# Five of the six slabs of the first in-projection by one level of Strassen's scheme, with the weight sums on GpSimd

## The chip, the cores and the metric

One Trainium2 chip, one of its cores. The metric is the device time of one execution of the whole kernel in microseconds (us). All data are float32.

## The reference, cut to what matters

One hybrid block: an input projection, two mixers (differential attention and a gated delta rule), a merge, 16 experts, and then a second block. The change touches only the first products of the input projection:

```
h = rmsnorm(x, norm1_w)              # 512 tokens x 1024
p = einsum('bsd,dn->bsn', h, w_in)   # w_in: 1024 x 9248
qa, ka, va = p[:, 0:1024], p[:, 1024:2048], p[:, 2048:3072]
qa = apply_rope(qa); ka = apply_rope(ka)     # t*cos + rot(t)*sin
# differential attention over qa, ka, va follows
```

## The kernel before, in words

The kernel is a row of blocks (`nc.Block`), each with a hand-written instruction order for every engine. Between two blocks all engines meet at a barrier. Inside a block an engine waits only on semaphores.

The first block (lines 241 to 414) makes `hT`, the normed input with the model dimension on the partitions (8 tiles `k` of 128, each 512 tokens wide), and the projections to `qa`, `ka` and `va`. The list `UNITS1` (line 239) has 24 units of work. A unit makes one 128 x 512 tile of output in a PSUM bank by 8 accumulating matmuls. The weights come as slabs of 1024 x 512 (2 MB), four units to a slab, six slabs in all: the first half of `va` (slab 4, four units), then `qa` and `ka` (slabs 0 to 3, sixteen units), then the second half of `va` (slab 5, four units). Two more slabs (6 and 7) are only loaded here, for the next block. The `v` units (line 328) hold a slice of `hT` as the stationary operand and stream 512 columns of the weights; the `qk` units (line 331) hold the weights and stream the 512 tokens of `hT`.

A float32 matmul is two passes in the trace: each has its own weight load (LDWEIGHTS) and its own MATMUL record, so a unit is 16 passes.

- TensorE takes the units in turn through four banks, `PS[n % 4]`. Unit n waits until the bank was emptied four units ago (`proj_evac`, line 312), and for its slab (line 315).
- ScalarE empties a bank into `raw` (line 366) or `va` (line 362). For `qk` it also copies the tile with the 32-row halves exchanged into `turned`, in four copies (line 368).
- VectorE makes the rotary form with three `tensor_tensor` instructions per unit (lines 407, 409, 411).
- GpSimd has four memsets at the start (line 292) and nothing else in this block. Its next work comes hundreds of us later.
- The DMA queue of SyncE loads slabs into four slots (`slab(i % 4)`). Slab i, from the fifth on, waits until the slot's units are done (line 285).

The next block (lines 437 to 604) is the attention. Its first matmul (line 455) needs `qT` and `kT`. Semaphores that are no longer used are collected in `spent`, cleared by GpSimd at the start of a later block (line 1448) and handed out again.

Of the kernel before, what the change touches and what calls it, by code (L numbers as in the profile page):

```python
# [110 lines left out]
def build(nc, io):  # L111
    ctx = ExitStack()
    counts = {}
    with ctx:
# [96 lines left out]
        def slab(slot, k=KD, cols=512):  # L211
            return SLB[slot][:, 0:k * cols].rearrange("p (k n) -> p k n", k=k)
# [20 lines left out]
        cosT, sinT = R[5][:, 0:S], R[5][:, S:2 * S]  # L233
        raw = [R[5][:, 1024 + i * S:1024 + (i + 1) * S] for i in range(2)]
# [4 lines left out]
        UNITS1 = [("v", 0, t) for t in range(NT)] + [("qk", u // 4, u) for u in range(NQK)] + [("v", 1, t) for t in range(NT)]  # L239
        SLABS1 = [4, 0, 1, 2, 3, 5, 6, 7]  # L240
        with nc.Block() as block:
            @block.sync
            def _(sp):
# [51 lines left out]
            def _(pe):  # L295
                def turn(t):
                    pe.wait_ge(tile_scaled, t + 1)
                    if t >= 2:
                        pe.wait_ge(hT_low, t - 1)
                        pe.wait_ge(hT_high, t - 1)  # L300
                    for k in range(KD):
                        m = pe.transpose(PS[4 + 2 * (t % 2) + k // 4][:, k % 4 * P:(k % 4 + 1) * P], hn[:, t, k * P:(k + 1) * P], ident)
                        if k % 4 == 3:
                            m.then_inc(tile_turned, 1)

                pe.wait_ge(ident_in, 16)
# [3 lines left out]
                for n, (kind, i, u) in enumerate(UNITS1):  # L310
                    if n >= 4:
                        pe.wait_ge(proj_evac, n - 3)
                    bank_ = PS[n % 4]
                    if n:
                        pe.wait_ge(slab_in[n // 4 % 4], 16 * (n // 16 + 1))
                    w = slab(n // 4 % 4)
                    if kind == "v":
                        if i == 0:
                            pe.wait_ge(hT_low, u + 1)
                        for k in range(KD):  # L320
                            if i == 0 and k == 4:
                                pe.wait_ge(hT_high, u + 1)
                            if n == 0 and k == 0:
                                pe.wait_ge(first_half, 16)
                            if n == 0 and k == 4:
                                turn(1)
                                pe.wait_ge(slab_in[0], 16)
                            m = pe.matmul(bank_[:, :], hT[:, k, u * P:(u + 1) * P], w[:, k, :], start=(k == 0), stop=(k == KD - 1))
                    else:
                        for k in range(KD):  # L330
                            m = pe.matmul(bank_[:, :], w[:, k, u % 4 * P:(u % 4 + 1) * P], hT[:, k, :],  # L331
                                          start=(k == 0), stop=(k == KD - 1))
                    m.then_inc(proj_done, 1)
                    if n < 2:
                        turn(n + 2)
                    if n == 8:
                        pe.wait_ge(rows_in, 16 * 7)
                        pe.transpose(PS[6][:, 0:120], rows[0:120, 0:P], ident[0:120, 0:120])
                        pe.transpose(PS[7][:, 0:30], rows[0:30, P:2 * P], ident[0:30, 0:30]).then_inc(vec_t, 1)
                pe.wait_ge(tab_in, 16)  # L340

            @block.scalar
            def _(act):
# [13 lines left out]
                for t in range(1, NT):  # L357
                    tile(t)
                for n, (kind, i, u) in enumerate(UNITS1):
                    act.wait_ge(proj_done, n + 1)  # L360
                    if kind == "v":
                        a(nc.scalar.activation(va[:, u, i * 512:(i + 1) * 512], PS[n % 4][:, :], ACT.Copy), proj_evac)
                        continue
                    if u >= 2:
                        act.wait_ge(rope_done, u - 1)
                    a(nc.scalar.activation(raw[u % 2], PS[n % 4][:, :], ACT.Copy), proj_evac)
                    for q in range(4):
                        a(nc.scalar.activation(turned[u % 2][32 * q:32 * q + 32, :], raw[u % 2][32 * (q ^ 1):32 * (q ^ 1) + 32, :], ACT.Copy),
                          raw_turned if q == 3 else None, q == 3)
                    if n == 9:  # L370
                        act.wait_ge(vec_t, 1)
# [6 lines left out]
            def _(dve):  # L378
# [18 lines left out]
                for t in range(1, NT):  # L397
                    scale(t)
                    weigh(t)
                dve.wait_ge(bc_in, 16 * 8)  # L400
# [4 lines left out]
                for u in range(NQK):  # L405
                    dve.wait_ge(proj_evac, NT + u + 1)
                    v(nc.vector.tensor_tensor(t1, raw[u % 2], cosT, ALU.mult))
                    dve.wait_ge(raw_turned, u + 1)
                    v(nc.vector.tensor_tensor(t2, turned[u % 2], sinT, ALU.mult))
                    dst = qT[:, u, :] if u < HEADS else kT[:, u - HEADS, :]  # L410
                    v(nc.vector.tensor_tensor(dst, t1, t2, ALU.add), rope_done)
                dve.wait_ge(lam_exp, 1)
# [227 lines left out]

        cut = [wab_[:, i * P:(i + 1) * P] for i in range(2)]
        with nc.Block() as block:
            @block.sync
            def _(sp):
# [731 lines left out]
        def expert_slab(eng, r):  # L1376
# [18 lines left out]
            for k in range(4):  # L1395
# [3 lines left out]

        spent.extend([proj_done, proj_evac, raw_turned, rope_done, score_done, max_ready,  # L1400
                      exp_done, pd_ready, pT_done, pT_ready, pv_done, oT_evac, rstd2, sq_ready, ss_done, norm_done,
                      cf_done, cf_evac, wab_in, ab_done, ab_evac, p3_done, conv_done, silu_done, sq3, ss3, rstd3, qk_norm,
                      tr3, tr3_evac, *pre.values(), *piece_in, first_done,
# [1229 lines left out]
```

## Time and profile before

| what | value |
|---|---|
| median of 3 runs | 2372.22 us (2370.93 to 2374.9) |
| span of the profiled execution | 2369.5 us |
| TensorE busy, share of the span | 93% |
| VectorE, ScalarE, GpSimd busy | 37%, 23%, 7% |
| first block, until the attention's first matmul | 181 us |

The page gives the span of the profiled execution alone, which runs from its first to its last instruction. The lowest of the three timed runs is 1.4 us above it, and their median 2.7 us. In a timeline row of the trace the first number is the start in us from the start of the span, the second how long the merged group lasts. MATMUL records overlap: one starts before the one before it has left the array, so the time that a pass costs is the distance between starts and not its own length.

### The profile page before, as it was taken

Reading aid. Unit: us, or ns where it says so; the run is one execution under the profiler, and the core shown is the slowest. Engines: PE = TensorE matmul, PEld = TensorE weight load, DVE = VectorE, ACT = ScalarE, POOL = GpSimd, SP = SyncE. Lnnn points to the kernel's source line nnn. Section 1 sums busy time; section 2 is a strip of 40 time slices with the busy share of each in tenths; the row PEclk is TensorE's granted clock in tenths of the full one; section 3 lists DMA queues with packets and bytes.
Section 4 is the critical chain, followed back from the end, with each engine's and each line's share of the span. In section 5 each row is a group of like instructions: output and inputs, shape, how many; then the busy total and the mean of one; then the engine's idle time right before and its main releaser. Section 6 shows DMA issues by size and latency. Waiting matters only on the chain. (4 is left out here: it accounts for less than half of the span.)

```text
span 2369.5 us, 28558 instructions
## 1 busy us (share of the span) xinstructions
PE 2211.2 (93%) x11793; PEld 1112.4 (47%) x11793; DVE 880.0 (37%) x1559; ACT 535.8 (23%) x1000; POOL 170.2 (7%) x166
## 2 busy tenths in 40 slices
PE   8999999999999999979999888888888888999998
PEld 4445554467777754434333333333333324455544
DVE  2327757665777640240101010101010102456764
ACT  2435645532222241010000000000000002233323
POOL 0000000043433300000000000000000000022000
PEclk9999999999999999989999999999999999999999
DMA  6212110011011152438999999999999997221210
GB/s 245 71 36 74 36 36 18 9 37 37 20 28 37 29 181 78 171 122 332 428 428 428 428 427 427 428 428 428 428 427 428 428 427 304 76 72 36 76 54 36
DMA packets 94115, 488.07 MB, mean 206 GB/s; under 512 B 9957, under 2 KB 36995, under 8 KB 68899
## 3 DMA queue, kind: packets, MB, share of 16 engines
q1 hardware_dynamic: 93987, 486.25, 50.7%
q8 instruction: 94, 1.54, 0.3%
q14 instruction: 34, 0.28, 0.0%
HBM read 482.82 MB, written 3.41 MB: 205 GB/s over the span
## 5 line engine op out<-in xcount | busy, mean ns | idle before, releaser
L1576 PE MATMUL PS<-R 128*64 128x512 f32 x1024 | 232.3, 601 | 31.9 <-DMA R<-w_up 24.6
L1576 PE MATMUL PS<-SL,R 128*64 128x512 f32 x1024 | 227.2, 595 | 25.7 <-DMA SL<-w_gate 17.8
L2069 PE MATMUL PS<-HT,SL 128*128 128x512 f32 x384 | 168.6, 594 | 0.0
L1768 DVE TENSOR_TENSOR HT<-HT,PS 128x512 f32<-128x512 f32 x32 | 20.6, 683 | 369.8 <-PE PS L1576 369.8
L1576 PEld LDWEIGHTS PS<-R 128*64 128x64 f32 x1024 | 70.6, 138 | 182.2 <-issue 127.5
L1576 PEld LDWEIGHTS PS<-SL,R 128*64 128x64 f32 x1024 | 72.6, 137 | 177.8 <-issue 128.1
L1605 PE MATMUL PS<-SL,HT 128*64 128x512 f32 x256 | 114.4, 594 | 14.7 <-issue 6.0
L1605 PE MATMUL PS<-R,HT 128*64 128x512 f32 x256 | 114.3, 594 | 12.5 <-ACT HT L1693 7.0
L1773 DVE COPY HT<-PS 64x512 f32<-64x512 f32 x16 | 10.9, 684 | 304.8 <-PE PS L1606 304.8
L1606 PE MATMUL PS<-SL,HT 128*64 128x512 f32 x256 | 114.9, 596 | 0.0
L1606 PE MATMUL PS<-R,HT 128*64 128x512 f32 x256 | 114.8, 595 | 0.0
L669 PE MATMUL PS<-HT,SL 128*128 128x512 f32 x256 | 113.9, 599 | 0.8 <-PEq L437 0.8
L2069 PEld LDWEIGHTS PS<-HT,SL 128*128 128x128 f32 x384 | 72.2, 190 | 87.2 <-issue 86.1
L961 PE MATMUL PS<-HT,X 128*128 128x512 f32 x256 | 112.5, 592 | 0.0
L1688 ACT ACTIVATE HT<-PS 128x512 f32<-128x512 f32 x32 | 17.4, 595 | 415.5 <-PE PS L1576 415.5
L331 PE MATMUL PS<-HT,SL 128*128 128x512 f32 x256 | 110.3, 592 | 0.0
L1895 POOL MEMSET R<- 64x512 f32 x1 | 0.5, 519 | 1163.1 <-POOLq L1405 1163.1
L331 PEld LDWEIGHTS PS<-HT,SL 128*128 128x128 f32 x256 | 48.6, 190 | 60.8 <-issue 60.7
L669 PEld LDWEIGHTS PS<-HT,SL 128*128 128x128 f32 x256 | 48.5, 192 | 58.7 <-issue 58.7
L961 PEld LDWEIGHTS PS<-HT,X 128*128 128x128 f32 x256 | 47.4, 190 | 53.6 <-issue 53.6
L1679 ACT ACTIVATE R<-PS 128x512 f32<-128x512 f32 x14 | 8.4, 597 | 271.3 <-PE PS L1550 271.3
L1605 PEld LDWEIGHTS PS<-SL,HT 128*64 128x64 f32 x256 | 33.6, 137 | 76.1 <-issue 70.8
(396 smaller groups left out, 3444.7 us busy)
## 6 DMA issues: line engine op xcount, KB each, us to landing
R<-w_gate SPq DMA_DIRECT2D x32, 2048.0 KB, 35.4
SL<-w_gate SPq DMA_DIRECT2D x32, 2048.0 KB, 33.6
SL<-w_up SPq DMA_DIRECT2D x32, 2048.0 KB, 32.7
R<-w_up SPq DMA_DIRECT2D x32, 2048.0 KB, 33.0
SL<-w_down SPq DMA_DIRECT2D x31, 2048.0 KB, 35.4
R<-w_down SPq DMA_DIRECT2D x28, 2048.0 KB, 27.8
SL<-w_in SPq DMA_DIRECT2D x18, 2048.0 KB, 8.2
X<-w_in SPq DMA_DIRECT2D x16, 512.0 KB, 3.8
```

The source lines that it names most:

```text
L331: m = pe.matmul(bank_[:, :], w[:, k, u % 4 * P:(u % 4 + 1) * P], hT[:, k, :], start=(k == 0), stop=(k == KD - 1))
L669: m = pe.matmul(PS[n % 4][:, :], slab(i)[:, k, j * P:(j + 1) * P], hT[:, k, :], start=(k == 0), stop=(k == KD - 1))
L961: m_ = pe.matmul(extra_bank(i)[:, :], piece[m % 2][:, k, :], src[:, k, :], start=(k == 0), stop=(k == KD - 1))
L1576: m = pe.matmul(banks[n][half * CAP:(half + 1) * CAP, :], XC[x // 2 % 2][:, 2 * j + k, toks], w[:, k, (2 * half + n) * 512:(2 * half + n + ...
L1605: pe.matmul(DB[0:CAP, :], hk, w[:, k, 0:512], start=first, stop=last)
L1606: m = pe.matmul(DB[CAP:P, :], hk, w[:, k, 512:1024], start=first, stop=last)
L1679: nc.scalar.activation(XC[q % 2][:, 4 * hf:4 * hf + 4, :], OB[hf][:, :].rearrange("p (k n) -> p k n", k=4), ACT.Copy).then_inc(E7["xc"], 1)
L1688: nc.scalar.activation(SG[j], GB[j][:, :], ACT.Silu).then_inc(E7["silu"], 1)
L1768: tt(H[:, j, :], SG[j], UB[j][:, :], ALU.mult).then_inc(E7["h"], 1)
L1773: nc.vector.tensor_copy(YP[rows, 0:512], DB[0:CAP, :])
L1895: g(nc.gpsimd.memset(ikz[0][64:128, :], 0.0), E9["ikpad"])
L2069: m = pe.matmul(bank_[:, :], slab(i % 2)[:, k, j * P:(j + 1) * P], hT[:, k, :], start=(k == 0), stop=(k == KD - 1))
```

## The change

Slabs 0 to 3 and 5 are no longer made by four units of 8 matmuls each. Contraction (1024), tokens (512) and columns of the slab (512) are halved, which would be eight quarter products; the scheme makes the slab from seven. A product is 8 float32 matmuls (two 128-row groups, four contraction tiles) that stream 256 columns, so 16 passes, and the two groups share a bank. The products M1, M6, M2, M7, M5, M4, M3 go in this order through two banks, and slabs take turns between the bank pairs 0/1 and 2/3. Some accumulate on the product before them in the bank.

- VectorE makes four sums of quarters of `hT` once (S1 to S4, 128 x 1024 elements each, into the free `R[2]`).
- GpSimd makes four sums of weight quarters per slab (T1, T2 in `R[6]`, and two in place in the slab), each 128 x 1024 elements.
- Per slab the PSUM results are taken out by two ScalarE copies (`one_` and the upper left quarter) and five VectorE additions of 128 x 512, one operand in PSUM. Before it was four ScalarE copies.
- The rotary steps of a slab are put between those of the next slab. `raw` moves from two tiles to two slabs' worth in `X`.
- GpSimd also clears 26 semaphores at the start of the third block: the five new ones, and 21 that before were cleared with the others in a later block.

The diff, cut to its core (the lines for the semaphores' lists and the unchanged code are left out):

```
+        SEVEN = 7
+        M1, M6, M2, M7, M5, M4, M3 = range(SEVEN)
+        OPENS = (M1, M6, M5)
+        def left_of(src, s1, s2, s3, s4):
+            return {M1: src[:, KLO, LO], M2: src[:, KHI, LO], M3: s4, M4: src[:, KHI, HI], M5: s1, M6: s2, M7: s3}
+        def right_of(w, t1_, t2_):
+            return {M1: w[:, KLO, LO], M2: w[:, KHI, LO], M3: w[:, KHI, HI], M4: w[:, KLO, LO], M5: t1_, M6: t2_, M7: w[:, KLO, HI]}
+        NST = 5
...
@@ sync
-                for i in range(4, 8):
-                    sp.wait_ge(proj_done, 4 * (i - 3))
+                sp.wait_ge(proj_done, NT)
+                weights(4)
+                for i in range(5, 8):
+                    sp.wait_ge(st_done, SEVEN * (i - 4))
                     weights(i)
@@ gpsimd
+                for i in range(NST):
+                    slot = (i + 1) % 4
+                    w = slab(slot)
+                    pool.wait_ge(slab_in[slot], 16 * ((i + 1) // 4 + 1))
+                    if i:
+                        pool.wait_ge(st_done, SEVEN * (i - 1) + M5 + 1)
+                    g(nc.gpsimd.tensor_tensor(T1_, w[:, KLO, HI], w[:, KLO, LO], ALU.subtract), st_t)
+                    g(nc.gpsimd.tensor_tensor(T2_, w[:, KHI, HI], T1_, ALU.subtract), st_t)
+                    g(nc.gpsimd.tensor_tensor(w[:, KLO, HI], w[:, KHI, HI], w[:, KLO, HI], ALU.subtract), st_t)
+                    pool.wait_ge(st_done, SEVEN * i + M1 + 1)
+                    g(nc.gpsimd.tensor_tensor(w[:, KLO, LO], w[:, KHI, LO], T2_, ALU.subtract), st_t)
@@ tensor
+                def product(i, p):
+                    slot = (i + 1) % 4
+                    x_, w = left1[p], right_of(slab(slot), T1_, T2_)[p]
+                    bank_ = PS[2 * (i % 2) + p % 2]
+                    if p == M1:
+                        pe.wait_ge(slab_in[slot], 16 * ((i + 1) // 4 + 1))
+                        if i >= 2:
+                            pe.wait_ge(st_dve, 5 * (i - 1))
+                        else:
+                            pe.wait_ge(proj_evac, NT)
+                    elif p == M6:
+                        pe.wait_ge(st_sum, 2)
+                        pe.wait_ge(st_t, 4 * i + 2)
+                    elif p == M2:
+                        pe.wait_ge(st_act, 2 * i + 1)
+                    elif p == M7:
+                        pe.wait_ge(st_sum, 3)
+                        pe.wait_ge(st_t, 4 * i + 3)
+                        pe.wait_ge(st_dve, 5 * i + 1)
+                    elif p == M5:
+                        pe.wait_ge(st_act, 2 * i + 2)
+                    elif p == M4:
+                        pe.wait_ge(st_t, 4 * i + 4)
+                        pe.wait_ge(st_dve, 5 * i + 2)
                     else:
+                        pe.wait_ge(st_sum, 4)
+                        pe.wait_ge(st_dve, 5 * i + 3)
+                    for g in range(2):
+                        cols = slice(g * P, (g + 1) * P)
+                        for k in range(K2):
+                            lhs, rhs = (w[:, k, cols], x_[:, k, :]) if i < NST - 1 else (x_[:, k, cols], w[:, k, :])
+                            m = pe.matmul(bank2(bank_[:, :])[:, g, :], lhs, rhs, start=(p in OPENS and g == k == 0), stop=(k == K2 - 1), skip_group_check=True)
+                    m.then_inc(st_done, 1)
@@ scalar
+                def turn_halves(u):
+                    if u >= 2:
+                        act.wait_ge(rope_done, u - 1)
+                    i, j = u // 4, u % 4
+                    act.wait_ge(st_dve, 5 * i + (4 if j < 2 else 5))
...
+                for i in range(NST):
+                    if i:
+                        turn_halves(4 * i - 4)
+                        act.wait_ge(st_dve, 5 * i - 1)
+                    act.wait_ge(st_done, SEVEN * i + M1 + 1)
+                    a(nc.scalar.activation(one_, bank2(PS[2 * (i % 2)][:, :]), ACT.Copy), st_act)
+                    if i:
+                        turn_halves(4 * i - 3)
+                        turn_halves(4 * i - 2)
+                    act.wait_ge(st_done, SEVEN * i + M2 + 1)
+                    if 2 <= i < NST - 1:
+                        act.wait_ge(rope_done, 4 * (i - 1))
+                    a(nc.scalar.activation(dest1(i)[0, 0], bank2(PS[2 * (i % 2)][:, :]), ACT.Copy), st_act)
+                    if i:
+                        turn_halves(4 * i - 1)
@@ vector
+                v(tt(S1_, hT[:, KLO, HI], hT[:, KHI, HI], ALU.add), st_sum)
+                v(tt(S2_, S1_, hT[:, KLO, LO], ALU.subtract), st_sum)
+                v(tt(S3_, hT[:, KLO, LO], hT[:, KLO, HI], ALU.subtract), st_sum)
+                v(tt(S4_, hT[:, KHI, LO], S2_, ALU.subtract), st_sum)
...
+                for i in range(NST):
+                    bank_a, bank_b = [bank2(PS[2 * (i % 2) + n][:, :]) for n in range(2)]
+                    to = dest1(i)
+                    if i:
+                        rope(4 * i - 4)
+                    dve.wait_ge(st_act, 2 * i + 1)
+                    dve.wait_ge(st_done, SEVEN * i + M6 + 1)
+                    v(tt(sixth, bank_b, one_, ALU.add), st_dve)
+                    if i:
+                        rope(4 * i - 3)
+                        rope(4 * i - 2)
+                    dve.wait_ge(st_done, SEVEN * i + M7 + 1)
+                    v(tt(seventh, bank_b, one_, ALU.add), st_dve)
+                    if i:
+                        rope(4 * i - 1)
+                    dve.wait_ge(st_done, SEVEN * i + M5 + 1)
+                    v(tt(to[1, 1], bank_a, seventh, ALU.add), st_dve)
+                    dve.wait_ge(st_done, SEVEN * i + M4 + 1)
+                    v(tt(to[1, 0], bank_b, one_, ALU.add), st_dve)
+                    dve.wait_ge(st_done, SEVEN * i + M3 + 1)
+                    v(tt(to[0, 1], bank_a, sixth, ALU.add), st_dve)
```

Here `rope(u)` is the three VectorE instructions of a unit as before, and `turn_halves(u)` the four copies of ScalarE as before.

## Rows read from the trace of the kernel before

**Rows 1.** Windows of the first block; columns: stretch, length, busy of PE, PEld, DVE, ACT, POOL, clock, DMA

```profile
41.90:69.40 27.50, 27.50 (x66) 12.19 (x65) 6.23 (x9) 9.91 (x16) 0.00 (x0) 1.00 0.22 76
96.90:124.40 27.50, 27.50 (x66) 12.19 (x65) 8.31 (x12) 12.42 (x20) 0.00 (x0) 1.00 0.21 76
```

**Rows 2.** Timeline of PE: 512-column passes, before the first qk unit and inside slabs

```profile
37.61 4.45 PE L328 MATMUL PS<-SL,HT 128*128 128x512 f32 x10
...
91.73 20.76 PE L331 MATMUL PS<-HT,SL 128*128 128x512 f32 x48
```

**Rows 3.** Two lines of PE: durations ns min/median/max of one record, first and last start

```profile
L331 PE MATMUL PS<-HT,SL x256: 592/592/697, 41.9 to 151.8; 128*128 128x512 f32 x128
...
L1935 PE MATMUL PS<-R,HT x64: 332/332/335, 2004.8 to 2017.3; 128*128 128x200 f32 x64
```

**Rows 4.** Waits: who waited for whom, total us, times, longest (SP's queue and PE)

```profile
SPq L1392 <- PE PS L1576: 501.9, 119, 12.4
...
PE PS L1576 <- DMA R<-w_up: 24.6, 23, 2.7
```

**Rows 5.** Timeline of PE around the second block's first norm: 200-column passes and 128-column ones

```profile
2008.43 2.87 PE L1935 MATMUL PS<-R,HT 128*128 128x200 f32 x16
2011.14 1.04 PE L1923 MATMUL PS<-tab,X 128*128 128x128 f32 x8
2012.01 5.58 PE L1935 MATMUL PS<-R,HT 128*128 128x200 f32 x32
```

**Rows 6.** Groups of weight loads by form: the 512-column stage and the 200-column one

```profile
L331 PEld LDWEIGHTS PS<-HT,SL 128*128 128x128 f32 x65 | 12.3, 190 | 15.5 <-issue 15.5
...
L1935 PEld LDWEIGHTS PS<-R,HT 128*128 128x128 f32 x64 | 10.7, 190 | 0.0
```

**Rows 7.** Timeline of PE: 256-column passes, each pair behind a wait of its own

```profile
2136.44 1.92 PE L1965 MATMUL PS<-R 128*128 128x256 f32 x6
2138.20 7.03 PE L2065 MATMUL PS<-SL,HT 128*128 128x512 f32 x16
...
2147.15 1.13 PE L1965 MATMUL PS<-R 128*128 128x256 f32 x4
2148.12 7.03 PE L2065 MATMUL PS<-SL,HT 128*128 128x512 f32 x16
```

**Rows 8.** Timeline: ScalarE's copy behind the fourth unit, and the attention's first matmul

```profile
42.16 0.60 ACT L362 ACTIVATE R<-PS 128x512 f32<-128x512 f32 x1 [6.27 <-PE PS L328]
...
181.04 1.99 PE L455 MATMUL PS<-R 64*128 64x512 f32 x8 [1.16 <-PEq L241]
```

**Rows 9.** Groups of GpSimd by form: line, operands, busy, mean ns of one

```profile
L1903 POOL TENSOR_TENSOR SL<-SL,R 128x1024 f32<-128x1024 f32 x7 | 22.6, 3232 | 128.3 <-ACT SL L2129 128.2
...
L1905 POOL TENSOR_TENSOR R<-R,SL 128x2048 f32<-128x2048 f32 x1 | 4.5, 4534 | 16.9 <-ACT SL L2182 16.9
```

**Rows 10.** Groups of ScalarE and VectorE by form in one slab's stretch, 96.9 to 124.4 us

```profile
L368 ACT ACTIVATE R<-R 32x512 f32<-32x512 f32 x16 | 10.0, 627 | 0.4
L407 DVE TENSOR_TENSOR R<-R 128x512 f32<-128x512 f32 x4 | 2.8, 693 | 10.9 <-ACT R L366 10.9
```

**Rows 11.** Timeline of DVE: end of the first norm, and one sum of 1024 elements elsewhere

```profile
28.00 1.42 DVE L391 TENSOR_TENSOR HT<-PS,small 128x512 f32<-128x512 f32 x2 [5.54 <-PE PS L302]
...
2100.42 1.22 DVE L2263 TENSOR_TENSOR SL<-R 128x1024 f32<-128x1024 f32 x1
```

**Rows 12.** Timeline of POOL and of DVE in the same 4 us of a later block

```profile
523.51 2.62 POOL L1191 TENSOR_TENSOR SL<-SL,R 128x512 f32<-128x512 f32 x2
...
523.52 0.69 DVE L1285 TENSOR_TENSOR SL<-PS,SL 128x512 f32<-128x512 f32 x1 [0.27 <-POOL SL L1188]
...
524.97 1.71 DVE L1268 TENSOR_TENSOR SL<-SL 128x512 f32<-128x512 f32 x1
```

**Rows 13.** One line of DVE: durations ns min/median/max, first and last start

```profile
L1268 DVE TENSOR_TENSOR SL<-SL x16: 691/694/1708, 521.8 to 837.7; 128x512 f32<-128x512 f32 x16
```

**Rows 14.** DMA issues of the first 50 us: KB each, median us to landing

```profile
SL<-w_in SPq DMA_DIRECT2D x4, 2048.0 KB, 13.5
```

More of the change, by code:

```diff
@@ L233, in build @@
         cosT, sinT = R[5][:, 0:S], R[5][:, S:2 * S]
-        raw = [R[5][:, 1024 + i * S:1024 + (i + 1) * S] for i in range(2)]
+        raw4 = [X[:, i * 2048:(i + 1) * 2048].rearrange("p (u s) -> p u s", u=4) for i in range(2)]
         turned = [R[5][:, 2048 + i * S:2048 + (i + 1) * S] for i in range(2)]
@@ L238, in build, with quarter, bank2, dest1 @@
         NQK = 2 * HEADS
-        UNITS1 = [("v", 0, t) for t in range(NT)] + [("qk", u // 4, u) for u in range(NQK)] + [("v", 1, t) for t in range(NT)]
         SLABS1 = [4, 0, 1, 2, 3, 5, 6, 7]
+        H2, K2 = S // 2, KD // 2
+        LO, HI, KLO, KHI = slice(0, H2), slice(H2, S), slice(0, K2), slice(K2, KD)
+        SEVEN = 7
+        M1, M6, M2, M7, M5, M4, M3 = range(SEVEN)
+        OPENS = (M1, M6, M5)
+        def quarter(reg, i):
+            return reg[:, i * K2 * H2:(i + 1) * K2 * H2].rearrange("p (k n) -> p k n", k=K2)
+        def left_of(src, s1, s2, s3, s4):
+            return {M1: src[:, KLO, LO], M2: src[:, KHI, LO], M3: s4, M4: src[:, KHI, HI], M5: s1, M6: s2, M7: s3}
+        def right_of(w, t1_, t2_):
+            return {M1: w[:, KLO, LO], M2: w[:, KHI, LO], M3: w[:, KHI, HI], M4: w[:, KLO, LO], M5: t1_, M6: t2_, M7: w[:, KLO, HI]}
+        def bank2(ap):
+            return ap.rearrange("p (g n) -> p g n", g=2)
+        NST = 5
+        S1_, S2_, S3_, S4_ = [quarter(R[2], i) for i in range(4)]
+        T1_, T2_ = quarter(R[6], 2), quarter(R[6], 3)
+        one_, sixth, seventh = bank2(R[6][:, 512:1024]), bank2(R[5][:, 1024:1536]), bank2(R[5][:, 1536:2048])
+        left1 = left_of(hT, S1_, S2_, S3_, S4_)
+        st_sum, st_t, st_done, st_act, st_dve = [sem(n) for n in ("st_sum", "st_t", "st_done", "st_act", "st_dve")]
+        def dest1(i):
+            if i < NST - 1:
+                return {(a, b): raw4[i % 2][:, 2 * b:2 * b + 2, (LO, HI)[a]] for a in range(2) for b in range(2)}
+            return {(a, b): va[:, 2 * a:2 * a + 2, 512 + b * H2:512 + (b + 1) * H2] for a in range(2) for b in range(2)}
         with nc.Block() as block:
@@ L309, in _ @@
                 turn(0)
[L310 to L328, printed above, removed]
-                    else:
[L330 to L336, printed above, removed]
@@ new lines, in _ @@
+                for t in range(NT):
+                    pe.wait_ge(hT_low, t + 1)
+                    w = slab(0)
+                    for k in range(KD):
+                        if k == 4:
+                            pe.wait_ge(hT_high, t + 1)
+                        if t == 0 and k == 0:
+                            pe.wait_ge(first_half, 16)
+                        if t == 0 and k == 4:
+                            turn(1)
+                            pe.wait_ge(slab_in[0], 16)
+                        m = pe.matmul(PS[t][:, :], hT[:, k, t * P:(t + 1) * P], w[:, k, :], start=(k == 0), stop=(k == KD - 1))
+                    m.then_inc(proj_done, 1)
+                    if t < 2:
+                        turn(t + 2)
@@ L337, in _ @@
+                for i in range(NST):
+                    for p in range(SEVEN):
+                        product(i, p)
+                    if i == 0:
                         pe.wait_ge(rows_in, 16 * 7)
@@ L358, in _ @@
                     tile(t)
[L359 to L363, printed above, removed]
+                for t in range(NT):
+                    act.wait_ge(proj_done, t + 1)
+                    a(nc.scalar.activation(va[:, t, 0:512], PS[t][:, :], ACT.Copy), proj_evac)
+                def turn_halves(u):
                     if u >= 2:
                         act.wait_ge(rope_done, u - 1)
-                    a(nc.scalar.activation(raw[u % 2], PS[n % 4][:, :], ACT.Copy), proj_evac)
+                    i, j = u // 4, u % 4
+                    act.wait_ge(st_dve, 5 * i + (4 if j < 2 else 5))
+                    r = raw4[i % 2][:, j, :]
                     for q in range(4):
-                        a(nc.scalar.activation(turned[u % 2][32 * q:32 * q + 32, :], raw[u % 2][32 * (q ^ 1):32 * (q ^ 1) + 32, :], ACT.Copy),
+                        a(nc.scalar.activation(turned[u % 2][32 * q:32 * q + 32, :], r[32 * (q ^ 1):32 * (q ^ 1) + 32, :], ACT.Copy),
                           raw_turned if q == 3 else None, q == 3)
-                    if n == 9:
+                for i in range(NST):
[13 more added lines that the diff above has]
+                        turn_halves(4 * i - 1)
+                    if i == 0:
                         act.wait_ge(vec_t, 1)
@@ L399, in _ @@
                     weigh(t)
+                tt = nc.vector.tensor_tensor
+                v(tt(S1_, hT[:, KLO, HI], hT[:, KHI, HI], ALU.add), st_sum)
+                v(tt(S2_, S1_, hT[:, KLO, LO], ALU.subtract), st_sum)
+                v(tt(S3_, hT[:, KLO, LO], hT[:, KLO, HI], ALU.subtract), st_sum)
+                v(tt(S4_, hT[:, KHI, LO], S2_, ALU.subtract), st_sum)
                 dve.wait_ge(bc_in, 16 * 8)
@@ L641, in build, with _ @@
         cut = [wab_[:, i * P:(i + 1) * P] for i in range(2)]
+        spent.extend([st_sum, st_t, st_done, st_act, st_dve, proj_done, proj_evac, raw_turned, rope_done, score_done, max_ready,
+                      exp_done, pd_ready, pT_done, pT_ready, pv_done, oT_evac, rstd2, sq_ready, ss_done, norm_done,
+                      cf_done, cf_evac, wab_in, ab_done, ab_evac])
         with nc.Block() as block:
+            @block.gpsimd
+            def _(pool):
+                clear_spent(pool)
             @block.sync
@@ L1398, in expert_slab @@
                 quarter_in.append((slab_in[4 + k], slab_n[4 + k]))
[L1400 to L1402 removed]
+        spent.extend([p3_done, conv_done, silu_done, sq3, ss3, rstd3, qk_norm,
                       tr3, tr3_evac, *pre.values(), *piece_in, first_done,
```

11 lines of the change are left out of this document (6 added, 5 removed).

## The prediction

> **What bounds the kernel now.** I read the page first: TensorE is busy for 93% of the span. I then cut the first block into windows of one slab each. In each (two of the five are shown) TensorE is busy for all of its 27.5 us, at full granted clock, while in these VectorE has at most 8.3 us of work, ScalarE 12.4, GpSimd none and the DMA engines a share of 0.22 [rows 1]. So the block lasts as long as its passes take, and only something that makes the passes fewer, shorter or later can move its end.
>
> How far apart passes start is in the timeline. 48 passes of 512 columns fill 20.76 us; taking off the last record's own length (592 ns, the median) and dividing by 47 gives 0.4291 us per pass [rows 2, 3]. A unit's sixteen passes are 6.87 us, and no gap shows where units and slabs meet.
>
> Is time saved here kept to the end? The waits say so. The slab loads wait for TensorE by the code (line 285), and the ring of expert slabs does so in the trace: 501.9 us in 119 waits [rows 4]. TensorE does wait for expert weights (24.6 us for one kind), but that stream starts when TensorE frees its room. An earlier start moves it as a whole. I count one us saved as one us.
>
> **The passes, the main term.** Twenty units of sixteen passes go: 320 x 0.4291 = 137.3 us. Five slabs of seven products of sixteen passes come: 560 passes of 256 columns. The price of such a pass decides the case, and the block has none. Elsewhere there are 32 passes of 200 columns in 5.58 us with real weights that change each time: (5.58 - 0.332) / 31 = 0.1693 us [rows 3, 5], where 0.332 is the length of one such record. Between 200 and 512 columns the slope is (0.4291 - 0.1693) / 312 = 0.833 ns per column, so 256 columns cost 0.1693 + 56 x 0.000833 = 0.2159 us. 560 of them are 120.9 us, and a product is 3.45 us. **Saved: 16.4 us**.
>
> The weight load is what could spoil it. It lasts 190 ns at 512 columns and the same 190 ns at 200, where the pass takes only 169 ns [rows 6]; so loads run under passes, and even under each other's. 256 columns leave more room than 200.
>
> The bound from the other side is a direct one: 256-column passes exist, in pairs with a wait in front of each pair. From 2147.15 four last until the next group starts at 2148.12, 0.2425 us each; from 2136.44 six last until 2138.20, 0.293 us each [rows 7]. The change waits only once in sixteen passes, as the 200-column groups do: one of those, sixteen passes behind a unit boundary, takes 2.71 us, again 0.169 each [rows 5]. So I take 0.2159 and keep 0.2425 and 0.293 for the range. The break-even, with the extra terms below, is (137.3 - 1.0) / 560 = 0.2434 us: only 27 ns per pass lie between gain and loss.
>
> **Start of the scheme.** M1 of the first slab waits until all four banks of the `va` units are empty; before, only the oldest had to be. The last of these passes ends at 42.06 us [rows 2], ScalarE begins its copy at 42.16 and takes 0.60 [rows 8], and with about 0.1 us back to TensorE, as from TensorE to ScalarE, M1 starts near 42.85 instead of 41.90. **Cost: 0.95 us**. If TensorE's queue hides part of it, it is nothing; it can't be more than the copy and two hand-overs by much.
>
> The sums S1 to S4 cost nothing there. VectorE is free at 29.4 us, and four sums at 1.22 us each end by 35 [rows 11]; M6 of the first slab comes at 46. T1 and T2 of it need two sums and the slab, which is among the first loads; those of its size land 13.5 us after their issue (median) [rows 14].
>
> **Cover inside a slab.** I lay the slab out from M1's start: M1 ends at 3.45, M6 6.9, M2 10.4, M7 13.8, M5 17.3, M4 20.7, M3 24.2.
>
> - GpSimd. A sum of 1024 elements costs between 2.27 us (half of the 2048-element one, 4.53) and 3.4 (the 1024-element ones average 3.23) [rows 9]. I take 2.3, since the quarters are rows of 256 and not short strips, and keep 3.4. T1 may begin when M5 of the slab before ends, and T2 must stand when M6 begins: M4, M3 and M1 lie between, 10.35 us, for two sums of 4.6 to 6.8. The third is due a product and more later, the fourth has from M1's end to M4's start, 13.8 us. All are covered; if they weren't, M6 would stall.
> - ScalarE. It does sixteen copies of 0.627 and two of 0.60 in 24.2 us, 11.2 in sum [rows 8, 10]. After M1's end: `one_` until 4.2, `turn_halves` twice until 9.4, then the M2 copy at 10.5, done at 11.2. M2 wants the first at 6.9, M5 the second at 13.8. Slack 2.6 us each.
> - VectorE. Twelve rotary steps of 0.69 and five additions of the same size make 12 us [rows 10, 11]. `sixth` is there at 7.7 for M7 at 10.4; `seventh` at 14.6 for M4 at 17.3; the M5 addition at 18.1 for M3 at 20.7. Slack 2.6 us each time. In the queue behind these waits stand rotary steps alone, which nobody on TensorE needs before the attention.
> - VectorE against GpSimd. Two rows speak against the change. While GpSimd worked on two SBUF operands (523.51 to 526.13), a VectorE addition with one operand in PSUM kept its 0.69 us, but one with both in SBUF took 1.71, ending after GpSimd's [rows 12]; this line is otherwise at 0.69 [rows 13]. So the new additions from PSUM are safe and the rotary steps are not: one can wait for a whole sum, 2.3 to 3.4 us. By the layout, three sums run from 17.4 to about 24.4 and the fourth from 3.5 to 5.9, while rotary steps stand at 0.7 to 2.9, 7.7 to 12 and 14.6 to 16.8. They hardly meet. With sums of 3.4 us the first rotary unit slides to about 8.3, `sixth` to 9.0, still ahead of 10.4. Cost nothing.
>
> The Trainium skill, "SBUF — State Buffer", section "SBUF: two separate sides", calls that port pair an exclusive lock, held for the full instruction while the other fully blocks; this trace agrees.
>
> - DMA. Even at 13.5 us a slab [rows 14] the loads are early: the tightest, the fifth of the scheme, is issued when the first's seven products are done and used three slabs, 72 us, later. Cost nothing.
> - Clears. GpSimd has no work in the block where it now clears 26 semaphores, nor did the later block wait for it. Cost nothing.
>
> **End of the block.** The last output is emptied by a VectorE addition of 0.69 us instead of a ScalarE copy of 0.60, behind which the barrier and the attention stand [rows 8, 11]: 0.1 us.
>
> **Sum.** -16.4 + 0.95 + 0.1 = -15.3 us. The span goes from 2369.5 to 2354.2 us. The three runs' median is 2.7 us above the profiled span; I put the same change on it: 2372.2 - 15.3 = **2356.9 us**. With 0.2% (4.7 us) as what a measurement of this kernel can tell, that is faster by 0.65%.
>
> **Rivals.**
>
> *Late sums (chance 0.09).* GpSimd becomes what M6 waits for. For: VectorE also holds GpSimd up, and both are fuller than before. Against: 3.5 us of room at the worst row. Were a sum 6 us, T1 and T2 would be 12.2 us, 1.85 late for each of four slabs: 7.4 us given back, 2364. To lose the whole gain, 3.8 per slab, a sum would have to take 7.1 us.
>
> *Short passes cost more (slower side, chance 0.05).* Place: each 256-column pass. If it costs the 0.293 us of the six paired ones, the 560 take 164.1 instead of 137.3 and the kernel ends at 2400. It decides from 0.2434 us per pass on. At 0.2425, the other row, the time is about 2372, no change (another 0.03). Against both: those passes had a wait each, and 200 columns cost 0.169 without one.
>
> *Weight loads not hidden at all (chance 0.01).* A load of 0.190 us ahead of each pass gives 0.406 us and 227 us for the 560, or 2463. The 200-column passes, shorter than their loads, speak against it plainly. The Trainium skill, "TensorE: Matmul & The Clock Gate", section "Measured speedup vs the span model", says that a weight load overlaps running matmuls only where the row groups differ, which full 128-row operands never do. By that rule this is the result. The trace contradicts it.
>
> *The gain is lost later (chance 0.03).* A transfer fixed in time would keep the later stages where they were: 2372. Against: the ring's waits are for TensorE [rows 4].
>
> **Numbers.** The forecast has 0.79. Faster by over 0.2%: forecast and most of the late sums, 0.87. Within: the 0.2425 case, the later loss and the worst late sums, 0.07. Slower: 0.06. The range begins at 2353, with no stall at the start (0.95) and runs that scatter by 2 to 3 us, and reaches to 2365, which takes in the late sums at 6 us.
>
> **What would show it.** Right: 560 passes of 256 columns, starts 0.216 us apart; slabs 24.2 us apart; one idle stretch of under 1 us before the first product; the attention's first matmul at 165.7 instead of 181.04; GpSimd sums of 2.3 to 3.4 us and no long wait of TensorE for them; some rotary steps stretched to 2 or 3 us. Wrong: a spacing of 0.24 or more, TensorE waiting for GpSimd's sums, or a gain at the attention's start that is not there at the end.

## The result and the profile after

| what | before | after |
|---|---|---|
| median of the runs of the first comparison | 2371.83 us (4 runs) | 2360.05 us (2358.54 to 2360.52, 4 runs) |
| ratio, 95% interval | | 0.9943 [0.9929, 0.9957] |
| span of the profiled execution | 2369.5 us | 2358.0 us |
| first qk pass, or first product | 41.90 us | 44.01 us |
| attention's first matmul | 181.04 us | 167.32 us |

The change is faster, by 11.8 us in the medians. The forecast was 15.3 us, the time 2356.9; 2360.05 lies inside the range of 2353 to 2365. In the traces the attention starts 13.7 us earlier, and the end of the span comes 11.5 us earlier.

The page of the changed kernel, busy time of each engine, and the granted clock in the forty slices (tenths of full clock):

```profile
PE 2197.4 (93%) x12033; PEld 1158.2 (49%) x12033; DVE 904.6 (38%) x1588; ACT 529.9 (22%) x990; POOL 217.5 (9%) x186
...
PEclk9999999999999999979999999999999999999999
```

The timeline of its TensorE through the block; the first row is the last two `va` units, each row of x16 one product, and the last row the attention:

```profile
29.27 13.90 PE L368 MATMUL PS<-SL,HT 128*128 128x512 f32 x32
44.01 3.69 PE L404 MATMUL PS<-HT,SL 128*128 128x256 f32 x16 [0.84 <-ACT R L435]
47.54 3.62 PE L404 MATMUL PS<-R 128*128 128x256 f32 x16
...
92.90 3.62 PE L404 MATMUL PS<-HT,SL 128*128 128x256 f32 x16
96.36 3.62 PE L404 MATMUL PS<-R 128*128 128x256 f32 x16
...
161.97 3.62 PE L404 MATMUL PS<-SL,R 128*128 128x256 f32 x16
167.32 1.99 PE L575 MATMUL PS<-R 64*128 64x512 f32 x8 [1.73 <-PEq L275]
```

Two products are 96.36 - 92.90 = 3.46 us apart, sixteen passes of 0.216 us. There is one idle stretch before the first product and one before the attention, and none between. That answers to [rows 2, 8].

GpSimd and VectorE of the same kernel. First the sums of one slab, then VectorE's rotary steps and its additions, by form, from 44 to 166 us:

```profile
86.33 2.35 POOL L335 TENSOR_TENSOR R<-SL 128x1024 f32<-128x1024 f32 x1 [11.18 <-PE PS L404]
88.76 2.36 POOL L336 TENSOR_TENSOR R<-SL,R 128x1024 f32<-128x1024 f32 x1
91.20 2.35 POOL L337 TENSOR_TENSOR SL<-SL 128x1024 f32<-128x1024 f32 x1
96.67 2.35 POOL L339 TENSOR_TENSOR SL<-SL,R 128x1024 f32<-128x1024 f32 x1 [3.12 <-PE PS L404]
```

```profile
L509 DVE TENSOR_TENSOR R<-R 128x512 f32<-128x512 f32 x16 | 13.1, 820 | 0.5
L505 DVE TENSOR_TENSOR R<-X,R 128x512 f32<-128x512 f32 x16 | 11.1, 692 | 0.5
```

A sum takes 2.35 us, a quarter less than the 1024-element rows and nearly as much per element as the 2048-element one [rows 9]. T2 stands at 91.1 us and M6 begins at 96.36: more than 5 us of room. One line of the rotary steps has a raised mean, 820 ns. Its cause is one instruction, held up by a sum:

```profile
L509 DVE TENSOR_TENSOR R<-R x16: 691/693/2732, 73.0 to 157.5; 128x512 f32<-128x512 f32 x16
```

It starts at 72.97 while T4 of that slab is under way (from 72.49, for 2.66 us), and nobody on TensorE waits for it.

### The profile page after: what moved, and what is told of

The parts are those of the page before. It is cut to its first block and busy times, and to the rows that moved or that the text cites. A ratio compares the mean times of both kernels' runs of the same rounds, so it can differ in the third digit from the quotient of the medians.

```text
span 2358.0 us, 29126 instructions
## 1 busy us (share of the span) xinstructions
PE 2197.4 (93%) x12033; PEld 1158.2 (49%) x12033; DVE 904.6 (38%) x1588; ACT 529.9 (22%) x990; POOL 217.5 (9%) x186
## 5 line engine op out<-in xcount | busy, mean ns | idle before, releaser
L2194 PE MATMUL PS<-HT,SL 128*128 128x512 f32 x384 | 168.6, 594 | 0.0
L796 PE MATMUL PS<-HT,SL 128*128 128x512 f32 x256 | 114.7, 602 | 0.8 <-PEq L557 0.8
L2194 PEld LDWEIGHTS PS<-HT,SL 128*128 128x128 f32 x384 | 72.2, 190 | 87.2 <-issue 86.1
L796 PEld LDWEIGHTS PS<-HT,SL 128*128 128x128 f32 x256 | 48.8, 194 | 59.3 <-issue 59.3
L1730 PEld LDWEIGHTS PS<-R,HT 128*64 128x64 f32 x256 | 33.5, 137 | 73.9 <-issue 70.4
L1768 PE MATMUL PS<-HT,R 128*128 128x512 f32 x112 | 53.9, 618 | 10.4 <-DVE HT L1899 10.4
```

The source lines that it names most:

```text
L796: m = pe.matmul(PS[n % 4][:, :], slab(i)[:, k, j * P:(j + 1) * P], hT[:, k, :], start=(k == 0), stop=(k == KD - 1))
L1730: pe.matmul(DB[0:CAP, :], hk, w[:, k, 0:512], start=first, stop=last)
L1768: pe.matmul(OB[half][:, :], STc[:, t, :], YP[:, half * 512:(half + 1) * 512], start=True, stop=True)\
L2194: m = pe.matmul(bank_[:, :], slab(i % 2)[:, k, j * P:(j + 1) * P], hT[:, k, :], start=(k == 0), stop=(k == KD - 1))
```

## The experiments

Where an experiment gives a distance, it is between two starts of TensorE in its trace. Every kernel ran beside the kernel before on the same chip; ratios are against that one. The four groups of runs did not see the same "before": its medians are 2371.83, 2376.14 (e1 to e4), 2375.84 (e5 to e8) and 2371.98 us (e9, e10). How much two traces of one kernel can differ shows below.

### e1: the changed kernel again, and e4: the kernel before again

Both are unchanged; they are there for second traces.

> The changed kernel once more, unchanged. In its first trace 1.1 us are missing before the scheme begins (the fourth unit's end) and 1.5 us around the end of the attention, where the granted clock is at half for 6.8 us instead of 2.9. Theory A (both are chance: where in the execution the clock rises and falls differs from run to run): the start of the scheme lies within 1.5 us of 43.0 and the low stretch behind the attention has another length than 6.8 us, so that the third block's shift against the kernel before differs from -12.2. Theory B (both belong to the change): start at 44.0 and a low stretch of 6.8 us again, within 0.3. Time by both 2360, within 1.5.

> The kernel before, unchanged, for a second trace of it. Theory A (the clock's moments are chance): the start of the first qk unit lies elsewhere than 41.90 by some tenths to 1.5 us, and the low stretch of the clock behind the attention is not 2.9 us long again. Theory B (they are fixed for a kernel): 41.9 and 2.9 within 0.3. Time 2372.

Measured: e1 2359.86 us (2358.74 to 2361.13), ratio 0.9929 [0.9917, 0.9942], which is 16.3 us in the medians. e4 2373.57 us, 0.9989 [0.9979, 0.9999], though it is the same kernel.

In e1 the first product starts at 43.26 instead of 44.01, and in e4 the first qk pass at 42.97 instead of 41.90. From there to the attention the distances repeat to 0.01 us: 123.31 in both traces of the changed kernel, 139.13 in both of the kernel before. So what comes ahead of the scheme is chance. The timelines show where: in the first eight passes of all. Before, then after the change:

```profile
10.00 5.40 PE L328 MATMUL PS<-SL,HT 128*128 128x512 f32 x8 [0.85 <-DMA SL<-w_in]
...
16.12 3.60 PE L328 MATMUL PS<-SL,HT 128*128 128x512 f32 x8
```

```profile
9.91 6.60 PE L368 MATMUL PS<-SL,HT 128*128 128x512 f32 x8 [1.24 <-DMA SL<-w_in]
...
17.22 3.60 PE L368 MATMUL PS<-SL,HT 128*128 128x512 f32 x8
```

The second eight take 3.60 us in both; the first eight take 5.40 and 6.60. The work around them is the same in both kernels. Their starts are 0.85 us apart at first and 0.43 later; four of the eight go at the slow pace before the change and seven after it. This is the clock too. The clock row reads full this early only because the traces have no clock record yet: the first one, at full clock, begins at 13.49 us in the first trace of before and at 15.81 in that of the change. In all twelve traces (13.47 to 16.55 us) it lies between the two starts where the pace changes.

The other place is the end of the attention. Granted clock in windows of 2 us there, the third block starting at 334.94 (before) and 321.81 (after); columns: stretch, length, PE busy (records), clock, DMA:

```profile
332.94:334.94 2.00, 1.16 (x11) 0.85 0.00 0
334.94:336.94 2.00, 2.00 (x3) 0.50 0.00 0
336.94:338.94 2.00, 2.00 (x5) 0.79 0.00 0
338.94:340.94 2.00, 2.00 (x6) 1.00 0.00 0
```

```profile
317.81:319.81 2.00, 2.00 (x19) 0.95 0.00 0
319.81:321.81 2.00, 1.16 (x6) 0.50 0.00 0
321.81:323.81 2.00, 2.00 (x3) 0.50 0.00 0
323.81:325.81 2.00, 2.00 (x4) 0.50 0.02 4
325.81:327.81 2.00, 2.00 (x5) 0.85 0.00 0
```

0.50 is 1.2 GHz, 1.00 is 2.4. TensorE issues 64 passes of 32 columns in front of the block's end. In the changed kernel the clock falls at 319.60 us, while they are still going (the last starts at 320.57), before the 0.84 us of the barrier. It is so in seven of the ten traces with these passes; in before, e2 and e3 it falls up to 0.9 us behind the start of the last one. At half clock it gets 3 records into 2 us where it else gets 5 or 6. By the trace's clock records the low stretch is 3.4 us long in the first trace of before (the expectations have 2.9) and 6.8 in that of after. e1 has 6.8 us as well, against theory A's guess of another length for the same kernel; but in e4 it is 10.2 us where the same kernel had 3.4 before. Theory A holds by e4, not by e1; e3 and e9 below are again one kernel, with 3.4 and 6.8 us. The distance from the attention's first matmul to the first one that puts expert outputs back in their places (line 1643 before the change; the expectations call it the first expert product) goes with it. On that way TensorE's instructions are the same in all kernels but e8 and e10:

| trace | low stretch behind the attention, us | attention to line 1643, us |
|---|---|---|
| before, e2, e3 | 3.4 | 996.9, 997.2, 997.5 |
| after, e1, e7, e9 | 6.8 | 999.1, 998.8, 998.5, 999.2 |
| e4, e5, e6 | 10.2 | 1001.8, 1000.9, 1002.2 |
| e8, e10 | none | 996.4, 996.0 |

(e4 and e6 have one more low stretch of 3.4 us on this way.) Each step costs some 1 to 2 us. 2.1 us between the two first traces come from here.

### e2: half as wide, without the scheme

```
-                            m = pe.matmul(bank_[:, :], w[:, k, u % 4 * P:(u % 4 + 1) * P], hT[:, k, :],
+                        for h in (slice(0, 256), slice(256, 512)):
+                            for k in range(KD):
+                                m = pe.matmul(bank_[:, h], w[:, k, u % 4 * P:(u % 4 + 1) * P], hT[:, k, h],
```

and the same for the last four `va` units, in the kernel before.

> The kernel before with each 512-column matmul of the twenty units replaced by two of 256 columns, so 640 passes of 256 columns instead of 320 of 512, with no scheme and no sums. Theory A (a pass of 256 columns costs 0.216 us, the weight load stays hidden): 138.2 us for the twenty units instead of 137.3, the kernel 0.9 us later than before, 2372.7 or no change. Rival (short passes pay extra and the scheme's products are cheap for some other reason): 0.2434 us or more per pass, the kernel 18 us or more later.

Measured: 2374.69 us, ratio 0.9993 [0.9984, 1.0002]. The twenty units and the way to the attention take 139.94 us instead of 139.13; the two ends of that way in TensorE's timeline:

```profile
42.81 34.70 PE L337 MATMUL PS<-HT,SL 128*128 128x256 f32 x160
...
182.75 1.99 PE L461 MATMUL PS<-R 64*128 64x512 f32 x8 [1.17 <-PEq L241]
```

With 320 passes at 0.4291 us taken off and 640 put on, a pass of 256 columns costs (137.31 + 0.81) / 640 = 0.2158 us. The groups of weight loads and matmuls by form, changed kernel, 41 to 165 us:

```profile
L404 PE MATMUL PS<-R 128*128 128x256 f32 x160 | 36.2, 379 | 0.0
...
L404 PEld LDWEIGHTS PS<-R 128*128 128x128 f32 x160 | 30.4, 190 | 4.1
```

A load lasts 190 ns where a pass takes 216: it is hidden. The rival of short passes that cost more falls, and so does the one of loads that don't overlap.

### e3: the two ends of the scheme

```
-                            pe.wait_ge(proj_evac, NT)
+                            pe.wait_ge(proj_evac, 2 * i + 1)
...
                     elif p == M6:
+                        if i < 2:
+                            pe.wait_ge(proj_evac, 2 * i + 2)
...
+                    if i == NST - 1:
+                        dve.wait_ge(lam_exp, 1)
+                        v(tt(lam[:, 0:1], lam[:, 2:3], lam[:, 3:4], ALU.subtract))
+                        v(nc.vector.tensor_scalar(lam[:, 0:1], lam[:, 0:1], LAMBDA_INIT, None, ALU.add))
                     dve.wait_ge(st_done, SEVEN * i + M3 + 1)
                     v(tt(to[0, 1], bank_a, sixth, ALU.add), st_dve)
```

The two lambda operations are taken from behind the loop.

> The changed kernel with two edits at the ends of the scheme: the first products of slabs 0 and 1 wait only for their own bank instead of all four, and the two small lambda operations go ahead of the last addition in VectorE's queue instead of behind it. Theory A (both lie on the path): the idle 0.84 us in front of the first product goes, and 0.37 us go between the last pass and the attention (1.73 us idle there becomes about 1.35); 1.2 us in sum, 2358.9. Rival (the barrier waits for something else, and the early start is caught up by the wait for the sums): no change, 2360.

Measured: 2357.58 us (2355.74 to 2358.77), ratio 0.9919 [0.9905, 0.9932], 2.3 us under e1 in the same group of runs. The end of the block in the changed kernel, then in e3 (timelines of all engines):

```profile
165.69 0.69 DVE L531 TENSOR_TENSOR R<-PS,R 128x512 f32<-128x512 f32 x1 [2.76 <-PE PS L404]
166.42 0.16 DVE L533 TENSOR_TENSOR small<-small 128x1 f32<-128x1 f32 x1
166.62 0.15 DVE L534 TENSOR_SCALAR small<-small 128x1 f32<-128x1 f32 x1
```

```profile
162.25 0.15 DVE L535 TENSOR_SCALAR small<-small 128x1 f32<-128x1 f32 x1
164.79 0.69 DVE L537 TENSOR_TENSOR R<-PS,R 128x512 f32<-128x512 f32 x1 [2.38 <-PE PS L406]
...
166.03 1.99 PE L578 MATMUL PS<-R 64*128 64x512 f32 x8 [1.34 <-PEq L275]
```

The idle time in front of the attention falls from 1.73 to 1.34 us. The first product now starts 0.43 us behind the last `va` pass, the plain distance of two 512-column passes, so the 1.01 us there are gone (43.00 would have been the next start in the changed kernel; 44.01 it was). The way from first product to attention is 122.85 instead of 123.31. Of the 2.3 us between the medians, 1.47 are these two edits. The other 0.8 are no more than the clock moves between runs (the trace of e3 has a low stretch of 3.4 us where that of e1 has 6.8, and that of e9, the same kernel as e3, has 6.8 too); that it made them is not shown.

### e5 and e6: more work on GpSimd

```
+                    for _ in range(1):
+                        g(nc.gpsimd.tensor_tensor(T1_, w[:, KLO, HI], w[:, KLO, LO], ALU.subtract))
+                        g(nc.gpsimd.tensor_tensor(T2_, w[:, KHI, HI], T1_, ALU.subtract))
                     g(nc.gpsimd.tensor_tensor(T1_, w[:, KLO, HI], w[:, KLO, LO], ALU.subtract), st_t)
```

e6 has `range(2)`.

> The changed kernel with T1 and T2 of every slab computed twice in a row on GpSimd: four sums of 2.42 us (with hand-over) instead of two between the end of M5 and the start of M6. Theory A (the cover is M4, M3 and M1, 10.35 us): 9.7 us still fit, by 0.6 us; the products stay 3.45 us apart and the attention starts 123.3 us after the first product, 2360. VectorE's rotary steps are stretched more often and longer. Rival (GpSimd and VectorE hold each other up on the way to TensorE's waits, so that the true slack is smaller): TensorE waits for VectorE or GpSimd in each slab, 1 us or more per slab, 2364 or more.

Measured: 2360.79 us; 123.30 us from first product to attention, and no wait for GpSimd. Here is what it did to the rotary steps:

```profile
L512 DVE TENSOR_TENSOR R<-R 128x512 f32<-128x512 f32 x16 | 19.2, 1200 | 0.5
L510 DVE TENSOR_TENSOR R<-R 128x512 f32<-128x512 f32 x16 | 18.9, 1179 | 0.9 <-ACT R L447 0.4
L508 DVE TENSOR_TENSOR R<-X,R 128x512 f32<-128x512 f32 x16 | 18.8, 1175 | 0.5
L526 DVE TENSOR_TENSOR R<-PS,R 128x512 f32<-128x512 f32 x5 | 3.5, 692 | 7.0 <-PE PS L407 6.9
```

All three lines rise from 0.69 (one of them 0.82) to nearly 1.2 us in the mean, and the additions from PSUM (L526) stay at 0.692. TensorE loses nothing, since it waits for the latter alone.

> The same with T1 and T2 three times: six sums, 14.5 us against a cover of 10.35. Theory A: TensorE waits about 4.2 us in front of M6 in slabs 1 to 4 (slab 0's are made long before), 16.7 us in all; the attention starts about 140 us after the first product, and the kernel ends at about 2377. Rival (smaller slack, as above): more than 20 us.

Measured: 2389.84 us, ratio 1.0063 [1.0045, 1.0081]; 151.91 us from first product to attention, 28.6 more than the change. The waits of TensorE, and its clock behind the first of them:

```profile
PE PS L407 <- POOL R L339: 19.9, 4, 5.1
```

```profile
76.00:78.00 2.00, 0.39 (x2) 1.00 0.05 17
78.00:80.00 2.00, 2.00 (x7) 0.50 0.00 0
80.00:82.00 2.00, 2.00 (x8) 0.65 0.00 0
82.00:84.00 2.00, 2.00 (x11) 1.00 0.00 0
```

It waits in the four slabs named, for T2. I had 4.2 us each and it is 5.0: the sums also lose a little to VectorE (2.67 instead of 2.35 us in two of the six, as the rotary steps ask for the port). The other 8.7 us are not waits. At the end of each of the four waits the granted clock falls to half for a while, 17 us in sum by the trace's clock records, and half of that is 8.5 us. The first product behind each wait takes 5.0 to 6.5 us instead of 3.45. So the total is that of the rival (more than 20 us), but not for its reason: the slack was as laid out, and I had left out what the clock does behind a wait. To overrun the cover costs nearly half as much again as the wait itself.

### e7: no GpSimd

```
                     v(tt(sixth, bank_b, one_, ALU.add), st_dve)
+                    weight_sums(i, 2)
...
                     v(tt(to[1, 1], bank_a, seventh, ALU.add), st_dve)
+                    if i + 1 < NST:
+                        weight_sums(i + 1, 0)
...
                     v(tt(to[1, 0], bank_b, one_, ALU.add), st_dve)
+                    if i + 1 < NST:
+                        weight_sums(i + 1, 1)
```

Part 0 is T1 and T2, part 1 the third sum, part 2 the fourth. GpSimd's loop is taken out, and the first slab's parts 0 and 1 stand ahead of VectorE's loop; the lines above leave both out.

> The changed kernel with all weight sums on VectorE instead of GpSimd, put behind the M6 and M5 additions (T4, T1 and T2) and behind the M4 addition (T3). A sum is 1.22 us there, so 4.9 us per slab on top of 12, in 24.2 us, and no two engines ask for the same port. Theory A (TensorE's passes alone set the block's length, and VectorE has room): first product to attention 123.3 us again, rotary steps at 0.69 without exception, 2360. Rival (the use of GpSimd is what makes the scheme pay, since VectorE is in line for TensorE's waits): TensorE waits for VectorE, 1 us or more per slab, 2364 or more.

Measured: 2360.14 us, ratio 0.9939 [0.9926, 0.9953]; 123.31 us, as with GpSimd. VectorE by form in this kernel:

```profile
L509 DVE TENSOR_TENSOR R<-X,R 128x512 f32<-128x512 f32 x16 | 11.1, 692 | 0.5
L497 DVE TENSOR_TENSOR SL<-SL,R 128x1024 f32<-128x1024 f32 x5 | 6.1, 1225 | 0.2
```

A sum takes 1.22 us there, and no rotary step is stretched. GpSimd is not what makes the scheme pay.

### e8: the clock behind the attention

On top of e3:

```
-                        m = pe.matmul(PS[4][:, t * 32:(t + 1) * 32], hT[:, k, t * P:(t + 1) * P], wab[:, k, :],
-                                      start=(k == 0), stop=(k == KD - 1))
+                        m = pe.matmul(PS[4][:, t * P:(t + 1) * P].rearrange("p (r n) -> p r n", r=4), hT[:, k, t * P:(t + 1) * P],
+                                      wab[:, k, :].unsqueeze(1).to_broadcast([P, 4, 32]), start=(k == 0), stop=(k == KD - 1))
```

and ScalarE takes the first of the four copies out.

> The kernel of e3_ends with one more edit at the attention's end: the 64 passes that stream 32 columns of the small projection stream the same 32 columns four times (128 columns); the copies go to unused parts of the bank. Such a pass costs 0.11 us either way. Theory A (the granted clock falls at the block's end because those passes keep TensorE nearly idle, and how long it stays low is chance: 3.4, 6.8 and 10.2 us in the five traces so far): with the wider passes no low stretch, or none over 3.5 us, starts within 10 us of the third block's start, 1.7 to 3.4 us faster than e3_ends, 2355 or less in the median. Rival (the clock falls because of the block's barrier, where TensorE is idle for 0.84 us): a low stretch as before, no change against e3_ends.

> The kernel of e3_ends again, beside e10_wide_repeat. By the theory that the low stretch behind the attention has a length of chance: a stretch of 3.4, 6.8 or 10.2 us there, and 997.2, 998.8 or 1000.9 us from the attention's first matmul to the first expert product accordingly (the traces so far lie within 0.3 us of these). Time 2356 to 2360.

> The kernel of e8_wide_ab again. Theory A (the 32-column passes let the clock fall): no low stretch at the third block's start again, 996.4 us on the same way within 0.3, and a median 1 to 3 us under e9_ends_repeat. Rival (its absence in e8_wide_ab was chance): a low stretch as in the others in this trace.

Measured: e8 2356.16 us (2354.85 to 2358.45), ratio 0.9922 [0.9908, 0.9936], 1.4 under e3 from another group of runs. In one group, e10 2355.80 us (2354.38 to 2358.16), 0.9931 [0.9919, 0.9944], and e9 2358.13 us (2356.87 to 2360.36), 0.9941 [0.9927, 0.9955]: 2.3 us less in the medians, with intervals that overlap. The clock of e8 around the third block's start (319.78), with the barrier in the first window:

```profile
317.78:319.78 2.00, 1.16 (x11) 1.00 0.00 0
319.78:321.78 2.00, 2.00 (x5) 1.00 0.00 0
321.78:323.78 2.00, 2.00 (x6) 1.00 0.02 4
```

The clock does not fall; nor does it in e10. The barrier, the same 0.84 us, is still there, and in seven traces the clock had fallen before it (above). So it was the 32-column passes. All ten traces of the other kernels have the low stretch, both traces with the wide passes have none. Two expectations were narrowly missed: e10 has 996.0 us to line 1643 where 996.4 within 0.3 was expected, and e9, with its 6.8 us stretch, 999.2 where it was 998.8 within 0.3. The passes themselves cost the same (TensorE's timeline of e8: 48 in 5.52 us; before the change 48 in 5.44). On the way to line 1643 the edit is worth about 1 us against the shortest low stretch and 4 to 6 against the longest (996.4 and 996.0 in the table). My 1.7 to 3.4 us holds for the pair e9 and e10, not for e3 and e8, and "2355 or less" was missed by one. e8 and e10 are faster than both kernels of the case.

## Why the prediction was right or wrong

**The passes: right.** 16.4 us were forecast, from 0.2159 us for a pass that the block did not have. It costs 0.2158 (e2). The interpolation between 200 and 512 columns held, and the 0.2425 and 0.293 of the paired passes [rows 7] were averages over starts that don't stand for the pass. The trace of before has the price itself, which the merged rows hide: of the four from 2147.15 the first start is 0.320 us ahead of the second, the other three distances are 0.215 to 0.216; of the six, two distances are 0.320, one is 0.470 with an idle gap, and three are 0.216. Read one by one, they would have given the answer without interpolation. That TensorE alone bounds the block is shown by e5 and e7: twice the sums, or the sums on another engine, and the same 123.3 us.

**The start of the scheme: right.** 0.95 us forecast, 1.01 in the trace, and e3 removes it.

**The cover inside a slab: right.** No product waits for a sum or an addition, at 2.35 us a sum. e5 and e6 put the edge where the layout has it (9.8 us of sums fit, six sums overrun), at somewhat over 10 us between the end of M5 and the start of M6.

**VectorE against GpSimd: the mechanism right, the cost nothing, as said.** One rotary step of 2.73 us in the changed kernel, and a mean of 1.2 us with the sums doubled, while the additions from PSUM keep 0.69.

**The end of the block: the term that was mis-sized.** "VectorE addition of 0.69 us instead of a ScalarE copy of 0.60 ... 0.1 us" was 0.57 (1.73 us idle against 1.16). The two lambda operations stand in the program behind the loop, as before. There they ran at 157 us, when the last rotary step was done and TensorE had 22 us to go:

```profile
157.26 0.16 DVE L413 TENSOR_TENSOR small<-small 128x1 f32<-128x1 f32 x1
```

Now the loop ends with the last addition, and they came behind it. I had counted the instructions that the change adds and not those that it leaves behind a later one. e3 takes 0.39 of it back.

**The sum.** Between the end of the `va` units and the attention the change saves 139.13 - 123.31 - 1.01 = 14.8 us, where 15.3 were forecast. The 0.47 us at the end are the difference. The attention starts at 167.32 instead of the 165.7 us of the prediction by these and by the 1.1 us of the first passes.

**From there to the end of the kernel.** "I count one us saved as one us" is right for queues and transfers: from line 1643 to the end both first traces take 1191.6 us. What the sum left out is that two executions of one kernel differ by as much as 6 us in places that the change does not touch. In the first pair of traces 1.1 us were lost in the first passes and 2.1 between the attention and line 1643, which leaves 11.6 of the 14.8, and the spans differ by 11.5; the spans of e4 and e1 differ by 18.5 us, with 0.7 and 3.0 us at the same places on top of the 14.8. The medians give 11.8 and 16.3 in two groups of runs; over all runs on record they are 2374.9 us (51 of the kernel before) and 2360.0 (9 of the changed one), 14.9 us apart, though the groups are not of one size. The first pair of spans came out 3.8 us under the forecast gain; 0.5 us of that are the end of the block, and 3.2 us are this chance.

The rivals: late sums, dear passes and unhidden loads did not occur, and no gain was lost to a transfer. The weight loads lie under matmuls of the same full row group. The rule that they overlap only where row groups differ stands in the Trainium skill, "TensorE: Matmul & The Clock Gate", in the section "The mechanism" (the prediction names the one behind it). It disagrees with the 0.2158 us beside a load of 0.190, and the measurement decides. The same section of the Trainium skill also lets a load go ahead into a background weight buffer, and with that the rows agree.

## What to carry to other kernels

Where one engine is busy without gaps, price its new instruction by the distance of starts in the nearest rows without waits, then lay out a period by hand and ask of each result when it stands and who takes it; here that came out to a few tenths of a us. Before interpolating a price, take a merged row apart: single starts may hold it. Look also for small instructions that the program leaves behind the loop: a loop that now ends later pushes them onto the barrier. When a change is worth less than 1%, compare the stretch that it touches and not only spans, since the granted clock alone moved spans of the same kernel by several us.

## What the runs showed that I had not expected

- 64 passes of 32 columns at a block's end let the granted clock fall to half (1.2 GHz), for 3.4, 6.8 or 10.2 us by chance, at 1 to 2 us a step. Streaming the same 32 columns four times costs nothing per pass (0.11 us) and kept the clock up in both traces.
- Four waits of 5 us on TensorE cost 28.6 us and not 20: at the end of each a stretch at half clock begins.
- The same kernel's distance between two fixed points repeats to 0.01 us over 139 us, while its span differs by 5.7 us (2369.5 and 2375.2).
